# Expert weights in 3 MB transfers: three units to a load, four semaphores in place of twelve

## The reference

```python
def expert_block(args):
    xb, e = args
    hh = jax.nn.silu(xb @ w_gate[e]) * (xb @ w_up[e])
    return hh @ w_down[e]
```

## Time and profile before

| | us |
|---|---|
| median of 3 runs | 1954.98 |
| the profiled execution, its own time | 1956.8 |
| its span | 1954.9 |
| TensorE (PE) busy | 1732.8 (89%) |
| VectorE (DVE) busy | 864.2 (44%) |
| ScalarE (ACT) busy | 627.6 (32%) |
| bytes moved | 526.35 MB, 269 GB/s over the span |
| expert transfers | 384, of 1024 KB each |

### The profile page before, as it was taken

The page is one execution under the profiler, slowest core; times in us unless marked ns, Lnnn a source line. Parts: engine busy times, 40 slices in busy tenths (PEclk is TensorE's granted clock), DMA queues, the critical chain, the costliest instruction groups (busy, mean ns, idle before and its releaser), DMA issues.

```text
span 1954.9 us, 31288 instructions
## 1 busy us (share of the span) xinstructions
PE 1732.8 (89%) x12626; PEld 1263.4 (65%) x12626; DVE 864.2 (44%) x1528; ACT 627.6 (32%) x1021; POOL 60.0 (3%) x58
## 2 busy tenths in 40 slices
PE   7999778788788899988878888899999989999997
PEld 7985334344245768543433433599888979998897
DVE  5642122122125644212212212469876555987654
ACT  4421111111113642201101111364447554543763
POOL 0200000000000010000000000100001200000110
PEclk9999998898898999988989989999999999998999
DMA  7638999999998313899999999544522334442222
GB/s 299 235 149 344 421 422 421 421 422 421 421 421 346 127 44 151 358 421 421 421 421 422 421 421 422 206 166 135 191 88 102 103 117 149 154 172 103 93 89 106
DMA packets 73091, 526.35 MB, mean 269 GB/s; under 512 B 8241, under 2 KB 8497, under 8 KB 9265
## 3 DMA queue, kind: packets, MB, share of 16 engines
q1 hardware_dynamic: 73008, 525.18, 67.3%
HBM read 524.10 MB, written 1.05 MB: 269 GB/s over the span
## 4 chain that ended last, share of the span: by engine, by line
PE 52%; DMA 27%; DVE 8%; SPq 7%; ACT 3%; issue 2%; POOL 0%; DVEq 0%; ACTq 0%
DMA arena<-experts 19%; PE banks L453 13%; PE banks L457 10%; PE banks L458 9%; PE banks L459 9%; SPq L412 7%; DMA ring<-experts 5%; PE banks L612 4%; PE banks L597 3%; PE banks L630 3%; DMA ring<-dense 2%; DVE arena L1429 2%; DVE ring_parts L1409 1%; DVE hT L1560 1%; ACT ring_parts L1016 1%
## 5 line engine op out<-in xcount | busy, mean ns | idle before, releaser
L457 PE MATMUL banks<-arena_parts,ring_parts 128*128 128x256 f32 (+1 forms) x1444 | 426.0, 295 | 28.0 <-DVE arena_parts L1424 13.2
L458 PE MATMUL banks<-arena_parts,ring_parts 128*128 128x256 f32 (+1 forms) x1444 | 415.1, 287 | 0.0
L459 PE MATMUL banks<-arena_parts,ring_parts 128*128 128x256 f32 (+1 forms) x1444 | 414.9, 287 | 0.0
L453 PEld LDWEIGHTS banks<-arena 128*128 128x128 f32 (+3 forms) x2704 | 342.9, 201 | 76.8 <-issue 60.9
L453 PE MATMUL banks<-arena 128*128 128x128 f32 (+5 forms) x2704 | 378.7, 298 | 13.4 <-DVE arena L1555 5.0
L1016 ACT ACTIVATE arena<-banks 128x256 f32<-128x256 f32 (+9 forms) x350 | 159.3, 485 | 462.4 <-PE banks L453 205.6
L457 PEld LDWEIGHTS banks<-arena_parts,ring_parts 128*128 128x128 f32 x1444 | 279.1, 193 | 39.5 <-issue 18.3
L1409 DVE TENSOR_TENSOR ring_parts<-ring,ring_parts 128x1024 fp32r<-128x1024 f32 x204 | 244.1, 1238 | 125.8 <-ACT ring_parts L1016 123.9
L612 PE MATMUL banks<-ring,arena 128*32 128x512 f32 x1536 | 210.3, 656 | 94.3 <-DMA ring<-experts 90.9
L458 PEld LDWEIGHTS banks<-arena_parts,ring_parts 128*128 128x128 f32 x1444 | 280.2, 194 | 0.1
L459 PEld LDWEIGHTS banks<-arena_parts,ring_parts 128*128 128x128 f32 x1444 | 279.5, 194 | 0.0
(11 more groups left out here) (208 smaller groups left out, 1614.2 us busy)
## 6 DMA issues: line engine op xcount, KB each, us to landing
ring<-experts SPq DMA_DIRECT2D x192, 1024.0 KB, 26.2
arena<-experts SPq DMA_DIRECT2D x160, 1024.0 KB, 20.8
ring<-dense SPq DMA_DIRECT2D x112, 1024.0 KB, 4.9
at<-experts SPq DMA_DIRECT2D x32, 1024.0 KB, 22.8
consts<-consts_in SPq DMA_DIRECT2D x1, 1414.0 KB, 13.7
vecs<-vecs_in SPq DMA_DIRECT2D x1, 1125.5 KB, 16.1
hT<-h_in SPq DMA_DIRECT2D x2, 544.0 KB, 4.6
out<-x SPq DMA_DIRECT2D x4, 256.0 KB, 2.3
```

Source lines behind the costliest of these rows:

```text
L453: return pe.matmul(o, lhsT, rhs, start=(k == 0), stop=(k == n - 1))
L457: pe.matmul(o, lhsT[0], rhs[0], start=(k == 0), stop=False)
L458: pe.matmul(o, lhsT[0], rhs[1], start=False, stop=False)
L459: return pe.matmul(o, lhsT[1], rhs[0], start=False, stop=(k == n - 1))
```

## The change

SP loads three units with one transfer wherever their slots lie side by side, and waits once for the three slots. Units 0 to 2, 3 to 5 and 6 to 8 are one transfer each, 9 and 10 are one of 2 MB, and unit 11, whose slot lies elsewhere, is one more that counts on the same semaphore. TensorE waits at units 0, 3, 6 and 9, at the last for 32 instead of 16. The early loads of the first quad go in threes too: behind dense units 3 and 6 in layer 0. The final state of the slots in `load_experts` is kept as it was.

```diff
+BY = 3
...
-        MOE = ("landed0 landed1 landed2 landed3 landed4 landed5 landed6 landed7 landed8 landed9 landed10 landed11 used "
+        MOE = ("landed0 landed1 landed2 landed3 used "
...
+        def expert_slots(n):
+
+            if n < RING // BY:
+                return ring[:, BY * n:BY * n + BY, :]
+            return more_slots[:, BY * n - RING:min(BY * n + BY, QU - 1) - RING, :]
...
-            def experts_first(layer, units):
-
-                for u in units:
-                    slot = u if u < RING else u - RING
-                    use = (free if u < RING else free_more)[slot]
-                    if use:
-                        sp.wait_ge(*use)
-                    sp.dma_start(expert_slot(u), experts[layer, 0, u]).then_inc(moe_sem[layer][f"landed{u}"], 16)
+            def load_three(layer, quad, n):
+
+                landed_n = moe_sem[layer][f"landed{n}"]
+                first, last = BY * n, min(BY * n + BY, QU - 1)
+                sp.dma_start(expert_slots(n), experts[layer, quad, first:last].rearrange("u p n -> p u n")).then_inc(landed_n, 16)
+                if last < BY * n + BY:
+                    sp.dma_start(expert_slot(last), experts[layer, quad, last]).then_inc(landed_n, 16)
+
+            def experts_first(layer, threes):
+
+                for n in threes:
+                    if n >= RING // BY:
+                        use = free_more[BY * n + BY - 1 - RING]
+                        if use:
+                            sp.wait_ge(*use)
+                    else:
+                        for u in range(BY * n, BY * n + BY):
+                            sp.wait_ge(*free[u])
+                    load_three(layer, 0, n)
...
-                experts_first(layer, range(RING))
+                experts_first(layer, range(RING // BY))
...
-                    for u in range(QU):
-                        sp.wait_ge(m["used"], i * QU + (u + 1))
-                        sp.dma_start(expert_slot(u), experts[layer, (i + 1) % QUADS, u]).then_inc(m[f"landed{u}"], 16)
+                    for n in range(QU // BY):
+                        sp.wait_ge(m["used"], i * QU + (BY * n + BY))
+                        load_three(layer, (i + 1) % QUADS, n)
...
-                if u < PAIRS_OF_SLOTS + QU - RING:
-                    experts_first(0, [RING + u - PAIRS_OF_SLOTS])
+                if u < PAIRS_OF_SLOTS + QU - RING and u % BY == 0:
+                    experts_first(0, [(RING + u - PAIRS_OF_SLOTS) // BY])
...
-            experts_first(1, range(RING, QU))
+            experts_first(1, range(RING // BY, QU // BY))
...
-                        pe.wait_ge(s[f"landed{u}"], i * 16 + 16)
+                        if u % BY == 0:
+                            of = 16 if u + BY < QU else 32
+                            pe.wait_ge(s[f"landed{u // BY}"], i * of + of)
```

## The result

| | before | after |
|---|---|---|
| median, all runs | 1958.83 us (10 runs) | 1972.43 us (10 runs) |
| range | 1951.87 to 1965.20 | 1967.92 to 1982.54 |
| ratio | | 1.0081, 95% interval 1.0061 to 1.0101 |
| the profiled execution | 1956.8 us | 1980.63 us |
| first L612 to last down products, layer 0 | 454.99 us | 462.57 us |

The account below looks back on a forecast made before the run. The expert stages were taken as bound by their transfer stream at 421 GB/s. Layer 0's 9.4 us, layer 1's 7.5 and the convolution's 0.3 made +17.2 us, 1972 us against the median of 1954.98; range 1957 to 1983.

Parts of the forecast that it names:

- The transfers cost nothing to merge, and nothing to keep apart: Steady expert stream: fewer, larger transfers save nothing; rate change taken as zero, at best 18.0 us less.
- No dry spell in the steady quads: Steady quads of both expert stages: queue never runs empty, margin 3.1 to 5.9 us, cost nothing.
- First refill: Start of each layer's expert stage: first refill issued once unit 2 is used, not unit 0; +1.8 us a layer.
- One dry spell: First quad of each layer: next trio waits for unit 8 in the down phase; +1.6 us layer 0, +1.2 layer 1.
- Both together in the landing of the last gate/up unit: Each layer's stream end: first refill and dry spell together delay the last gate/up landing, +3.4 and +3.0 us.
- Units 6 and 7 and the lower clock: Last quad of each layer: both units multiplied together after unit 8 lands, at lower clock; +3.5 us layer 0, +1.95 layer 1.
- The convolution: Early expert loads in threes behind dense units 3 and 6 delay dense units 4 and 7; +0.3 us, bounds 0 to 3.
- The signs of being wrong: Steady quad's period leaving 29.86 us, or the last quad starting its preparation less than 4 us later.
- B: Streamed expert units: fewer transfer switches raise the rate, so the kernel is not slower; 1954 us if all comes; chance 0.14.
- D: Merged transfers: alternating rows from three units lower the rate; 1% gives 1981 us, 3% gives 1999; chance 0.04.
- C: Steady quads: queue runs dry in every quad; 2000 us at one microsecond beyond the margin; chance 0.05.
- E: Below the program, merged transfers are cut into single units again, only waits change; same sum as the forecast; chance 0.03.

Follow-up runs that it names:

- single-transfer kernel: Waits and releases in threes as in the changed kernel, but every unit its own 1 MB transfer on the shared semaphore; 1.0091 against the kernel before.
- busy kernel: The changed kernel with five idle matmuls of 512 columns before TensorE's wait at unit 6; 1.0132 against the kernel before.
- halves: As the changed kernel, but units 0 to 5 in one 6 MB transfer, 6 to 10 in one of 5 MB with unit 11 behind; 2177.11 us, ratio 1.1112.
- release-only kernel: The kernel before, with only SyncE waiting for the last unit of each three before issuing three refills; 1.0035 against the kernel before.

## Why the prediction was right, point by point

- **What bounds the stage**: the bytes, at 421 GB/s in both kernels and in the single-transfer kernel. Held.
- **The transfers cost nothing to merge, and nothing to keep apart**: held, within 1.4 us over both loops. The rule of the Trainium skill, "DMA: Bandwidth & Descriptors", section "Anatomy of one DMA", that the semaphore write is nearly free, agrees; the page gives it for transfers issued by GpSimd, and these are issued by SyncE.
- **No dry spell in the steady quads**: held, 29.86 us a quad.
- **First refill, +1.8 us**: the refill is issued 155.65 - 152.60 = 3.05 us after the first L612, before it was 1.33: +1.7.
- **One dry spell, +1.6 and +1.2 us**: 1.4 and 1.2 by the bytes.
- **Both together in the landing of the last gate/up unit**: forecast +3.4 and +3.0 us. Measured, after taking off the 2.49 us between units 7 and 8: +2.0 and +3.6. The terms are right as SP issues the refills; what TensorE meets at the other end differs by 1.4 us down and 0.6 up. That comes from landings that lag their bytes by different amounts, in the first quad already, and the cause is open (see the last section).
- **Units 6 and 7 and the lower clock, +3.5 and +1.95 us**: from landing to down products +3.1 and +1.3. The busy kernel showed the mechanism in layer 0: 2.3 of the 3.1 us are the clock's, and the 0.9 left is the one more unit.
- **The convolution, +0.3 us**: undersized. Dense unit 4 landed 9.9 us after its issue and not 8.9, and TensorE waited 1.2 us for the first half of a split that it had not waited for. Whether this reaches the total is not shown: the first expert matmul starts at 152.60 us against 152.92 before, and in the kernels that kept the old convolution at 152.15 to 153.58. The line of the changed kernel's waits:

```profile
PE banks L475 <- DVE ring_parts L1429: 1.2, 1, 1.2
```

- **The sum**: +17.2 us forecast; the loops as measured make 15.0, with the wait in the convolution at most 16.2, and the ratio says 15.9 (interval 11.9 to 19.8). The mechanism is the one forecast. That 1972 met the median of 1972.43 is partly luck: the base of 1954.98, the median of three executions, was 3.9 us below the 1958.83 of ten, and the forecast change was 3.6 us above the 13.6 between the medians (1.3 above the 15.9 of the ratio). The two errors cancel. The upper end of the prediction's own range is added up too high, too: its bounds for clock and convolution lead from 1972 to 1978 and not to 1980. The 1.93 us for which SP is blocked at a unit stand in the chain of the kernel before (231.39 us and on), not in the earlier trace rows; nothing hangs on them.
- **The signs of being wrong**: neither came. The steady period stayed, and the last quad's preparation starts 7.0 us later after the first L612 (603.64 - 152.60 against 596.92 - 152.92), where less than 4 would have spoken against it. The last L650 of layer 0 is 7.3 us later, for about 9 forecast.

Of the rivals, B and D fell with the single-transfer kernel, C with the steady period. E falls by the packets that the pages of the profiles count: the changed kernel has 4656 packets under 512 B, the one with single transfers under the same waits 8240, which is 16 fewer for each of the 224 transfers saved, while the packets of 8 KB and more are as many (63825 in both). The merged transfers stay merged. C's mechanism is real, as the halves showed, only not at this depth.

## What to carry to other kernels

In this stream, which already fills the DMA engines with 1 MB transfers, 3 MB transfers gain nothing, while coarser waits cost at the stream's two ends: later first refills, and a last step that starts when the whole group has landed. Waits so coarse that the queue runs out cost in every step, as the halves did. If loads must be grouped, cut the groups where the consumer's phases change; a group that spans two phases holds free slots until the later phase and holds up the earlier one. Look instead at what stands behind the last landing: work there that doesn't need it can go into the pauses ahead of it, which here gave 0.4%.

## What was not expected of the hardware

- Landing times do not follow from bytes alone. In the changed kernel, the first 3 MB after the dry spell landed 9.77 us after the issue in layer 0 and 12.21 in layer 1, though 7.47 us of transfer were to be done and, as an estimate from the windows, only some 0.3 us of older transfers were left in layer 0 and about 1 us in layer 1. The layer kept that lag to its end. Units 6 and 7 of the second quad start 29.30 and 31.38 us after the first L632, those of the last quad 447.40 and 449.14: between them lie 418.10 and 417.76 us, fourteen periods of 29.86 (418.0) within 0.3 us. The single-transfer kernel does the same. Its second quad of layer 0, in the chain:

```profile
185.35 3.23 PE banks L630 x16
```

That is 30.81 us after its first L630 and 418.03 before the last quad's start; in layer 1 they are 31.21 and 418.15 us. By the prediction's own terms (issue after 3.05 us, 2.4 more to the first byte, nine units of 2.49, the dry spell as measured) this landing was due after 29.3 and 29.1 us in the changed kernel, so it is 0.0 and 2.3 us behind its bytes. The kernel before, taken back in the same way from its last landing, was some 1.2 us behind in both layers. This is what the last-landing terms above miss, and it is as large as single terms of the sum. Some engines being behind the others would look like this; the runs don't show it, and it stays open.
- The clock can give back what a stream loses. The same unit and preparation took 1.06 + 5.56 us in the release-only kernel and 1.93 + 6.42 in the kernel before, at the end of layer 1, so the kernel with the later stream had the shorter layer end. What set the level in each case was not tested there.
